# The scratch layout of the expert gates turned from one block per slab of keys to one block per group of tokens

## The reference

```
def peer_ffn(h, wq, keys, u_tab, v_tab):
    q = (hc @ wq).reshape(PEER_BLOCK, PEER_HEADS, 2, PEER_DHALF)
    sc = jnp.einsum('thcd,hckd->thck', q, keys)
    s1, i1 = lax.top_k(sc[:, :, 0], PEER_TOPK)
    s2, i2 = lax.top_k(sc[:, :, 1], PEER_TOPK)
    ...
    gate = jax.nn.softmax(top, axis=-1)
    ue = jnp.take(u_tab, eidx, axis=0)
    act = jax.nn.gelu(jnp.einsum('thkd,td->thk', ue, hc))
    ve = jnp.take(v_tab, eidx, axis=0)
    return jnp.einsum('thk,thkd->td', (gate * act), ve)
```

## Time and profile before

| quantity | value |
|---|---|
| median of three runs | 3917.6 us |
| profiled execution | 3911.64 us |
| its span, first to last instruction | 3909.9 us |
| PE busy | 3664.4 us (94%) |
| DVE busy | 2947.6 us (75%) |
| ACT busy | 1353.3 us (35%) |
| bytes moved by DMA | 876.27 MB, mean 224 GB/s |

### The profile page before, as it was taken

One profiled execution on the slowest core, in us unless ns is written; L12 is line 12 of the kernel. 1 busy time (PEld: TensorE's weight loads), 2 busy tenths in 40 slices (PEclk: granted clock), 3 DMA queues, 4 the chain that ended last, 5 costly groups with the idle time before them and its releaser, 6 DMA issues. The chain is left out here.

```text
span 3909.9 us, 69568 instructions
## 1 busy us (share of the span) xinstructions
PE 3664.4 (94%) x28586; PEld 3349.7 (86%) x28586; DVE 2947.6 (75%) x5404; ACT 1353.3 (35%) x2055; POOL 634.6 (16%) x592
## 2 busy tenths in 40 slices
PE   8798889899999999999989888989999899999998
PEld 5568767799998999999976776669999899999998
DVE  7576464588998987888866646458899898788886
ACT  3431233333334433333333123333333344333332
POOL 2000000022221132232300000002212112233231
PEclk9899999999999999999999999999999999999999
DMA  7720222288887899999941031227788789999995
GB/s 233 268 65 31 98 69 72 91 258 252 254 263 235 295 335 330 368 360 359 359 157 65 3 116 44 97 83 244 247 255 253 230 299 324 337 358 358 359 359 180
DMA packets 323805, 876.27 MB, mean 224 GB/s; under 512 B 29696, under 2 KB 158848, under 8 KB 315680
## 3 DMA queue, kind: packets, MB, share of 16 engines
q1 hardware_dynamic: 249760, 603.36, 45.5%
q0 software_dynamic: 73728, 268.47, 19.0%
HBM read 746.93 MB, written 124.78 MB: 223 GB/s over the span
## 5 line engine op out<-in xcount | busy, mean ns | idle before, releaser
L217 PE MATMUL peer_ps<-peer_h_high,tile_high 128*128 128x384 f32 (+1 forms) x2304 | 797.6, 346 | 51.0 <-ACT up_act L2342 21.0
L219 PE MATMUL peer_ps<-peer_h_high,tile_low 128*128 128x384 f32 (+1 forms) x2304 | 787.7, 342 | 0.0
L218 PE MATMUL peer_ps<-peer_h_low,tile_high 128*128 128x384 f32 (+1 forms) x2304 | 787.5, 342 | 0.0
L210 DVE TENSOR_TENSOR tile_low<-tile,tile_high 128x1024 fp32r<-128x1024 f32 x544 | 663.0, 1221 | 141.1 <-ACT tile_high L205 126.1
L217 PE MATMUL peer_ps<-gate_high,tile_high 128*128 128x384 f32 x2048 | 690.7, 337 | 7.8 <-DVE tile_low L210 7.8
L218 PE MATMUL peer_ps<-gate_low,tile_high 128*128 128x384 f32 x2048 | 690.3, 337 | 0.0
L219 PE MATMUL peer_ps<-gate_high,tile_low 128*128 128x384 f32 x2048 | 690.0, 337 | 0.0
L2222 POOL DMA_INDIRECT row<-in_peer_u_rows,row_at x256 | 314.7, 1229 | 1774.4 <-DVE row L2466 1050.6
L205 ACT ACTIVATE tile_high<-tile 128x1024 fp32r<-128x1024 f32 x544 | 571.2, 1050 | 21.6 <-DMA tile<-in_peer_u 21.3
L217 PEld LDWEIGHTS peer_ps<-peer_h_high,tile_high 128*128 128x128 f32 x2304 | 434.2, 188 | 77.9 <-issue 45.3
L219 PEld LDWEIGHTS peer_ps<-peer_h_high,tile_low 128*128 128x128 f32 x2304 | 434.5, 189 | 10.7
(11 more groups left out here) (480 smaller groups left out, 5200.5 us busy)
## 6 DMA issues: line engine op xcount, KB each, us to landing
tile<-in_peer_u SPq DMA_DIRECT2D x256, 512.0 KB, 4.7
tile<-in_peer_v SPq DMA_DIRECT2D x256, 512.0 KB, 5.6
gates<-gates_out SPq DMA_DIRECT2D x24, 2048.0 KB, 11.8
gates_in<-gates SPq DMA_DIRECT2D x32, 1536.0 KB, 9.5
acts<-up_act SPq DMA_DIRECT2D x240, 192.0 KB, 5.0
act_in<-acts SPq DMA_DIRECT2D x240, 192.0 KB, 5.9
in_w<-in_w_in SPq DMA_DIRECT2D x36, 512.0 KB, 3.4
tile<-in_peer_wq SPq DMA_DIRECT2D x32, 512.0 KB, 3.8
```

Source lines behind the costliest of these rows:

```text
L210: return dve.tensor_tensor(out, value, high.bitcast(F32), ALU.subtract)
L217: pe.matmul(out, wh, mh, start=first, stop=False)
L218: pe.matmul(out, wh, ml, start=False, stop=False)
L219: return pe.matmul(out, wl, mh, start=False, stop=last)
```

## The change

The DRAM array `gates` held for each slab of 8 keys one block [128 partitions, 12 groups of tokens, 8 x 32 values]. It now holds for each group of 32 tokens one block [128 partitions, 128 keys, 32 values]. The store of a group was scattered in 16 pieces of 1 KB for each partition; it is now one piece of 16 KB. The load of a slab was one piece of 12 KB for each partition; it is now 12 pieces of 1 KB, which lie 2 MB apart, and those of neighbouring partitions lie 16 KB apart. SBUF tiles, their contents, and all waits are the same.

```
             def store_gates(n):
                 sp.wait_ge(gates_taken.sem, gates_taken.at(8 * (n + 1)))
-                sp.dma_start(gates[:, :, n, :].rearrange("s p f -> p s f"),
-                             spill[n % 2][:, :, :].rearrange("p (s k) t -> p s (k t)", k=SLAB)).then_inc(gates_stored[n % 2].sem, 16)
+                sp.dma_start(gates[n], spill[n % 2][:, :, :]).then_inc(gates_stored[n % 2].sem, 16)
...
-                sp.dma_start(slabs[s % NSLAB][:, :, :], gates[DOWN[s * SLAB] // SLAB]) \
+                first = DOWN[s * SLAB]
+                sp.dma_start(slabs[s % NSLAB][:, :, :], gates[:, :, first:first + SLAB, :].rearrange("g p k t -> p g (k t)")) \
...
-    dram["gates"] = nc.dram_tensor("gates", (SLABS, P, TD // SPILL, SLAB * SPILL), F32, kind="Internal").ap()
+    dram["gates"] = nc.dram_tensor("gates", (TD // SPILL, P, NKEY, SPILL), F32, kind="Internal").ap()
```

## The result

The kernel after took 3958.86 us (median of 4 runs, 3948.75 to 3967.38), beside 3917.51 us for the kernel before (4 runs by now, 3911.64 to 3917.97). The ratio is 1.0112 with a 95% interval of [1.0092, 1.0134]: slower, where I had 3923.6 us and a range up to 3939 us. The profiled execution took 3949.28 us with a span of 3947.6 us, 37.7 us longer than before, and about 10 us under its own median.

The account below looks back on a forecast made before the run. PE was taken to set the pace of spread and down stages, with DMA full at the handoffs. Terms -2 + 8 + 0 = +6 us on the median 3917.6 gave 3923.6 us, range 3911 to 3939.

Parts of the forecast that it names:

- The handoff, +8 us: Between spread and down stages: gathered rows pass the slab, the tile behind it comes late; +4 us a layer, +8 together.
- The down stage, 0 us: Down stages: with the slab last in turn, tiles lose at most about 1 us, hidden by PE's three buffers; 0 us.
- the prediction's own signs of being wrong: Slabs alone far under 388 GB/s, PE idle in the down stage, or q0 and q1 sharing by bytes.
- The price of 1 KB loads, +0.12 us a slab: Slab loads: 4.05 us in small pieces against 3.93 in large; 0.2 us over both handoffs, rounded away.
- The stores, -2 us: Spread stages: larger gate stores finish earlier, so the tile and acts store behind come earlier; -2 us, between 0 and 4.2 gained.
- DMA bound: Rival: DMA share of 0.94 to 0.96 is already the wall, so each of 28 slabs costs; 3935 us, chance 0.13.
- Slow pieces: Rival: 1 KB loads suffer from their addresses, a slab takes 8.1 us, down stage just full; 3940 us, chance 0.12.
- Its small case: Slow-pieces rival with loads suffering 14% only: +1.3 us.

Follow-up runs that it names:

- The late slab 0: Slab 0 issued after the up stage's last two tiles: on the kernel after with split slabs, ratio 1.0016 to before; on the kernel before, 0.9976.
- the split: Kernel after, with each down-stage slab load issued as four DMAs, one after each of four tile loads; 3922.69 us, ratio 1.0051 to before.
- the second queue: Kernel after, with down-stage slab loads issued by ScalarE in its own queue instead of by SyncE; 3921.75 us, ratio 1.0030 to before.
- the last experiment: Kernel after, without the 128 gathers per layer of in_peer_v in the down stage; 3927.92 us, one run.
- the near pieces: Layout of before with gaps, so a slab load reads 12 pieces of 1 KB per partition, 1.25 KB apart; 3943.49 us, ratio 1.0103 to before.
- the padded layout: Kernel after with 10 unused keys per partition, so partitions lie 17.25 KB and groups 2.2 MB apart; 3936.9 us, ratio 1.0087 to before.

## Why the prediction was wrong

- **The handoff, +8 us: right in its mechanism, and in its size partly by luck.** It grew by 3.7 and 6.9 us, where I had 4 and 4. The mechanism was read correctly: equal packet counts, rows first, the tile behind the slab late, and one wait of PE of 8.15 us. But the rows that passed were 3.51 MB where they had been 2.03, 2.8 gathers more and not five, and all queues together moved 4.51 MB in that stretch where they had moved 4.73. So one term of the working was too large and the slower transfer was left out; that the two partly cancelled is argued, not measured. The late slab 0 shows that the tile was late for the slab's place in the queue, and also that moving the slab does not free the handoff of the new layout: 3.9 and 3.4 us stay, as DVE's wait for the slab itself.
- **The down stage, 0 us: this step failed.** It is the step "rows gain and tiles lose at most about 1 us, and PE's three buffers hide it". It measured +29.4 us. I used the same turn of the queues at the handoff and then did not carry it into the down stage. No row stands behind the "about 1 us"; the one stretch of slab that I had read there, has no gather in it. Yet a slab that moves slowly meets gathers: each row buffer that DVE frees starts another, which passes with about four times the slab's bytes. The slab's landing went from 9.5 to 14.5 us, and a tile behind it came about 8.5 us late, where its cover was about 5.0 us. The slowed clock behind the waits was no term of the sum either. That PE idles in the down stage was one of the prediction's own signs of being wrong. The runs showed the three parts one by one, by the length of the down stages: with 4 KB packets the loss goes (533.6 us), with no gathers it goes (533.7 us), and with the tile out of line it goes (533.6 us, by the split and by the second queue).
- **The price of 1 KB loads, +0.12 us a slab: too low.** From 1718 to 1719 us the slab was almost alone in the kernel after, and moved at 354 GB/s; in the last experiment it had 265. At 265 GB/s a slab takes an estimated 1.57 / 0.265 = 5.9 us, where I had 4.05. I had taken 388 from stores in 1 KB pieces, and in neither stretch did the loads reach it. The next row shows the stretch at 354:

```profile
DMA packets 345, 0.35 MB, mean 354 GB/s; under 512 B 2, under 2 KB 344, under 8 KB 345
```

- **The stores, -2 us: at most 0.9.** Landing fell from 11.8 to 10.5 us, and the spread stages nearly kept their length (197.4 to 196.5 us, 196.6 in both in layer 2). PE idled only 2.4 and 1.8 us there before, so there was little to win.
- **The rivals.** "DMA bound" gave 3935 us and a slower kernel, for a reason that the split refutes. "Slow pieces" named the right order (3940 us) by addresses; the near pieces refute the addresses as the main cause, though slower pieces by themselves are a part of it. Its small case has a slip as well: with 14% only, four slabs would cost 2.5 us and not 1.3. The right case was a fifth one: the forecast's own mechanism, at work in both stages. It would have been 28 more chances to be late, beside the two handoffs; 11 of them cost PE a wait in the traced execution.
- **The pitch and the turns.** No effect of the 2 MB between pieces stands out here: the padded layout gave 1.0087 beside 1.0112, intervals overlapping, and the pieces 1.25 KB apart gave 1.0103. The Trainium skill, page "DMA: Bandwidth & Descriptors", says in "Latency and other measured facts" that tiles whose partitions lie 2 MiB apart in HBM were copied at 164 GB/s, against 207 at 512 KiB. That is another shape than this one, where partitions lie 16 KB apart and only the pieces of one partition 2 MB. On the turns, q0 and q1 finished 970 and 968 packets, and 968 packets held 0.99 MB, so each 1 KB piece is a packet of its own in the trace. The same page of the Trainium skill, section "Queues, rings and completion order", has an engine go round the queues packet by packet, with a packet usually of 9 to 17 descriptors. The counts agree with the turns, and no bundling to equal bytes is seen here.

## What to carry to other kernels

When two DMA queues are busy, compare the sizes of their packets, because in these traces a queue's share of the bytes followed them and not its need. Then look at what stands in line behind the transfer with the small packets, and count how often that happens in each stage, not only where the engine idles today. A large background load belongs behind the urgent tiles, in pieces between them, or in another queue.

## What the runs showed that I had not expected

- SP can be held up by issuing. Beside a slab in 1 KB pieces, the issue of one activation load took up to 4.43 us in the down stage of layer 1, where it took at most 0.33 us before. The loads behind it, tiles among them, are issued later for it. First before, then after:

```profile
L2188 SPq DMA_DIRECT2D act_in<-acts x115: 319/320/327, 1504.2 to 1978.1; - x115
```
```profile
L2188 SPq DMA_DIRECT2D act_in<-acts x112: 319/320/4429, 1503.2 to 1986.8; - x112
```

- POOL's gathers of `in_peer_v` took 1531 ns on average instead of 1145, and 1140 again with the split slabs (times on POOL are rough). The row of the kernel after (391.9 is the busy time in us of all 256):

```profile
L2222 POOL DMA_INDIRECT row<-in_peer_v,row_at x256 | 391.9, 1531 | 636.5 <-DVE own_sum L2472 564.6
```

- A DMA share of 0.99 over 460 us went with a PE that never idled. The share says how busy the engines look, not whether the urgent transfer comes in time.
